# Pages spread over their ring slots by quarters, query products per column tile, scores and rope turned on VectorE, pair sums on column tiles

## What is computed

```python
def page_block(phys):
    kn, kr, v = mla_keys(cache_l[phys], w_uk, w_uv, k_norm_nope)
    return partial_softmax(mla_scores(qn, qr, kn, kr), v)
# kn = rms_norm(c @ w_uk) per head; scores = (qn . kn + qr . kr) * scale, over 8 heads
# partial_softmax: maximum over the tokens, exp, sum, and the sum weighted by v
```

## Time and profile before

| | |
|---|---|
| median of 3 runs | 1494.56 us |
| the profiled execution, its own time | 1494.17 us |
| its span, first to last instruction | 1492.4 us |
| PE busy | 1482.2 us, 99% |
| ACT busy | 880.6 us, 59% |
| DVE busy | 814.0 us, 55% |
| POOL busy | 216.6 us, 15% |
| share of PE in the chain that ended last | 96% |
| granted TensorE clock, mean | 0.999 |
| the page loop, first to last page's keys | 0.10 to 1.15 ms |

### The profile page before, as it was taken

One profiled execution on the slowest core, in us unless ns is written; L12 is line 12 of the kernel. 1 busy time (PEld: TensorE's weight loads), 2 busy tenths in 40 slices (PEclk: granted clock), 3 DMA queues, 4 the chain that ended last, 5 costly groups with the idle time before them and its releaser, 6 DMA issues.

```text
span 1492.4 us, 26962 instructions
## 1 busy us (share of the span) xinstructions
PE 1482.2 (99%) x9284; PEld 1221.2 (82%) x9284; DVE 814.0 (55%) x1596; ACT 880.6 (59%) x2836; POOL 216.6 (15%) x111
## 2 busy tenths in 40 slices
PE   9999999999999999999999999999999999999998
PEld 7877777867878778778777777778777999999998
DVE  5854444555455563555554555635433766787543
ACT  5545667686566675576855666755766454344332
POOL 3001111111131111111222111111312000000000
PEclk9999999999999999999999999999999999999999
DMA  9542315632245433255322463332644465555551
GB/s 284 169 116 36 77 44 125 157 82 61 63 99 135 114 81 73 60 127 135 83 61 61 101 151 80 63 68 61 162 106 121 149 211 206 168 171 176 185 183 58
DMA packets 263714, 173.92 MB, mean 117 GB/s; under 512 B 165464, under 2 KB 212088, under 8 KB 263448
## 3 DMA queue, kind: packets, MB, share of 16 engines
q1 hardware_dynamic: 263266, 171.94, 44.2%
q10 hardware_dynamic: 318, 0.33, 0.1%
HBM read 132.63 MB, written 6.74 MB: 93 GB/s over the span
## 4 chain that ended last, share of the span: by engine, by line
PE 96%; DVE 2%; ACT 1%; issue 0%; POOL 0%; DVEq 0%; ACTq 0%
PE ps L1991 17%; PE ps L1993 16%; PE ps L1992 16%; PE ps L2400 5%; PE ps L2401 5%; PE ps L2402 5%; PE ps L2031 2%; PE ps L2012 2%; PE ps L2084 2%; PE ps L2348 2%; PE ps L2349 2%; PE ps L2085 2%; PE ps L2086 2%; PE ps L2350 2%; PE ps L2150 2%; PE ps L2162 1%
## 5 line engine op out<-in xcount | busy, mean ns | idle before, releaser
L846 ACT ACTIVATE ksq<-ps 128x128 f32<-128x128 f32 x1024 | 268.9, 277 | 304.8 <-PE ps L1993 303.1
L1991 PE MATMUL ps<-ukh,cTh 128*128 128x512 f32 x1024 | 418.5, 409 | 0.3 <-DVE cTl L1233 0.3
L1993 PE MATMUL ps<-ukh,cTl 128*128 128x512 f32 x1024 | 401.3, 392 | 0.0
L1992 PE MATMUL ps<-ukl,cTh 128*128 128x512 f32 x1024 | 400.0, 391 | 0.0
L700 POOL TENSOR_TENSOR rk<-kss,mhalf 128x32 f32<-128x32 f32 x32 | 179.5, 5609 | 502.8 <-DVE kss L1659 502.8
L1991 PEld LDWEIGHTS ps<-ukh,cTh 128*128 128x128 f32 x1024 | 192.5, 188 | 55.4 <-issue 17.3
L1993 PEld LDWEIGHTS ps<-ukh,cTl 128*128 128x128 f32 x1024 | 192.2, 188 | 43.1
L1992 PEld LDWEIGHTS ps<-ukl,cTh 128*128 128x128 f32 x1024 | 192.9, 188 | 34.3
L846 ACT ACTIVATION_READ_ACCUMULATOR ksq<-ps 128x1 f32 x1024 | 211.6, 207 | 0.0
L834 ACT ACTIVATE cTr<-turned 128x1024 uint16<-128x1024 uint16 x126 | 173.6, 1378 | 9.6 <-PE ps L2015 6.9
L1035 ACT ACTIVATE wh<-wraw 128x2048 fp32r<-128x2048 f32 x44 | 84.3, 1916 | 131.7 <-PE ps L2402 127.2
(11 more groups left out here) (501 smaller groups left out, 2697.9 us busy)
## 6 DMA issues: line engine op xcount, KB each, us to landing
clat<-cache_mla SPq DMA_DIRECT2D x128, 256.0 KB, 2.6
wraw<-w_in SPq DMA_DIRECT2D x16, 1024.0 KB, 5.2
wraw<-w_up SPq DMA_DIRECT2D x16, 1024.0 KB, 5.4
wraw<-w_down SPq DMA_DIRECT2D x16, 1024.0 KB, 5.1
braw<-w_in SPq DMA_DIRECT2D x24, 512.0 KB, 4.0
crope<-cache_mla SPq DMA_DIRECT2D x128, 32.0 KB, 2.4
sst<-state_gdn SPq DMA_DIRECT2D x32, 128.0 KB, 3.2
gdn_sample<-sst SPq DMA_DIRECT2D x32, 128.0 KB, 2.1
```

The source lines that it names most:

```text
L846: i = nc.scalar.activation(ksq[:, P * h:P * h + P], ps[:, k % 3, P * h:P * h + P], ACT.Square, accum_out=kss[:, n // 4 % 2, n % 4, 4 * hal ...
L1991: mm(out, cTh[:, n % 2, c], ukh[:, c, cols], start=c == 0, stop=False)
L1992: mm(out, cTh[:, n % 2, c], ukl[:, c, cols], start=False, stop=False)
L1993: i = mm(out, cTl[:, n % 2, c], ukh[:, c, cols], start=False, stop=c == 3)
```

## The change

Five things are changed.

1. **Layout of the ring.** The four pages of a group are spread over the group's four slots: page `q` goes to partitions 32q to 32q+31 of all four, and slot `j` holds tokens 32j to 32j+31 of each page. Each load thus writes 32 partitions. One semaphore per group of slots counts all eight loads (`group_landed`).
2. **Scores.** `query_products` has for each latent chunk `c` four products, one per page `q` in column tile `q` (8 weight columns, 128 moving columns, 16 in all, the chunks summed in PSUM), and for the rope part eight with 32 rows each (`qro`). The result stands so that turning blocks of 32x32 gives a token to a partition: DVE does that in `score_parts` with one transpose straight from PSUM. `score_rows` (ACT) and `score_columns` (PE) are gone.
3. **Rope.** DVE `turned_rope` turns the rope part in blocks of 32x32 from `crope` to `rpT`; `rope_columns` (PE) and its copy (ACT) are gone. The queries' part `qro` is made once by 16 small products in `front_pe(2)`; two DMAs and a memset go.
4. **Places.** `split_planes` for page n+2 comes right behind `split_lo(n + 1)` in page n; it was at the end of page n-1. `turn` moves by one half page with it, the page loads from `i % 8 == 3` to 2, and `weigh` from the start of page t = 1 to the middle of page t = 0.
5. **Pair sums.** `l2r` and `osr` put each product's sum into a column tile of its own (32 weight columns), so the rows lie 32 apart, and `lb` is spread with 128 weight rows, `ob` with 64.

The diff, cut to its core:

```diff
-        qeff, e = place("qeff", [P, NS, 5, 16], F32, taken["rsq"][0])
+        qeff, e = place("qeff", [P, NS, 4, H], F32, taken["rsq"][0])
+        qro, e = place("qro", [P, NS, 2, H], F32, e)
         idr, e = place("idr", [P, P], F32R, e)
...
-        stp = ps[:, B_SCORE, :].rearrange("p (t n) -> p t n", t=4)
+        sparts = prows[:].rearrange("p (y x j r) -> p y x j r", y=2, x=2, j=4)
...
             def page(u, n):
                 pg = sp.value_load(ptab[0:1, bass.ds(n, 1)] if not isinstance(n, int) else ptab[0:1, n:n + 1], min_val=0, max_val=I["cache_mla"].shape[1] - 1)
                 rows_ = I["cache_mla"][0][bass.ds(pg, 1), :, :].rearrange("o p n -> p (o n)")
-                sp.dma_start(clat[:, u, :], rows_[:, 0:LAT]).then_inc(S(f"page_landed{u}"), 16)
-                sp.dma_start(crope[:, u, :], rows_[:, LAT:LW]).then_inc(S(f"page_landed{u}"), 16)
+                q, slots = u % 4, slice(u - u % 4, u - u % 4 + 4)
+                sp.dma_start(clat[32 * q:32 * q + 32, slots, :], rows_[:, 0:LAT].rearrange("(j a) n -> a j n", a=32)).then_inc(S(f"group_landed{u // 4}"), 16)
+                sp.dma_start(crope[32 * q:32 * q + 32, slots, :], rows_[:, LAT:LW].rearrange("(j a) n -> a j n", a=32)).then_inc(S(f"group_landed{u // 4}"), 16)
             def turn(n):
...
             sp.dma_start(O["conv_sample"][0, :, 0:CONVW - 2, :], I["state_conv"][0, :, 1:CONVW - 1, :]).then_inc(S("conv_shift"), 16)
             for i in range(2 * NT):
-                n = (i - 3) // 2 + RING - 8
-                if i % 8 == 3 and i >= 16 and n < NT:
+                n = (i - 2) // 2 + RING - 8
+                if i % 8 == 2 and i >= 16 and n < NT:
                     sp.wait_ge(S("pv_used"), i // 8 - 1)
                     for m in range(n, n + 4):
                         page(m % RING, m)
-                if i % 2 == 0 and i // 2 + 2 < NT:
+                if i % 2 == 1 and i // 2 + 2 < NT:
...
-            def turned_rope(gg):
-                act.wait_ge(S("rope_done"), gg + 1)
-                wait(act, "qk_done", gg)
-                nc.scalar.activation(rpT[:], ps[:, B_SCORE, 0:2 * P], ACT.Copy).then_inc(S("rope_ready"), 1)
-            def score_rows(gg):
-                act.wait_ge(S("qk_done"), gg + 1)
-                wait(act, "st_done", gg)
-                nc.scalar.activation(prows[:], ps[:, B_SCORE, :], ACT.Copy).then_inc(S("ssb_ready"), 1)
...
-                if t == 2:
-                    turned_rope(g)
-                if t == 3:
-                    score_rows(g)
                 beside(2 * n)
...
-            v.wait_ge(S("pool_clear"), 4)
+            v.wait_ge(S("pool_clear"), 3)
             def split_planes(n):
...
+            def turned_rope(gg):
+                wait(v, "qk_done", gg)
+                u = 4 * (gg % 3)
+                V.transpose(rpT[:], crope[:, u:u + 4, :].rearrange("p j n -> p (j n)")).then_inc(S("rope_ready"), 1)
             def score_parts(gg):
-                v.wait_ge(S("st_done"), gg + 1)
-                V.tensor_reduce(sparts[:, gg % 2].rearrange("p t a h -> p t (a h)"), stp.rearrange("p t (c n) -> p t n c", c=4)[:, :, 0:16, :], AX, ALU.add).then_inc(S("s_parts"), 1)
+                v.wait_ge(S("qk_done"), gg + 1)
+                V.transpose(sparts[:, gg % 2].rearrange("p x j r -> p (x j r)"), ps[:, B_SCORE, 0:256]).then_inc(S("s_parts"), 1)
...
+                V.tensor_tensor(ssc[:, y], sparts[:, y, 0, :, 0:H], rk[:, y], ALU.mult).then_inc(S("s_half"), 1)
...
-                V.tensor_tensor(ssc[:, y], sparts[:, y, :, 1, :], ssc[:, y], ALU.add).then_inc(S("s_ready"), 1)
+                V.tensor_tensor(ssc[:, y], sparts[:, y, 1, :, 0:H], ssc[:, y], ALU.add).then_inc(S("s_ready"), 1)
...
+                    V.tensor_scalar(lr[:, 0], bank("l2r")[:, 0:T], 1.0, EPS, ALU.mult, ALU.add).then_inc(S("a_read"), 1)
                 if k == 16:
...
                 if n + 1 < NT:
                     split_lo(n + 1)
+                if 1 <= n < NT - 2:
+                    split_planes(n + 2)
+                if t == 2:
+                    turned_rope(g)
                 if t == 0 and g >= 1:
                     score_parts(g - 1)
...
                 beside(2 * n + 1)
-                if n + 3 < NT:
-                    split_planes(n + 3)
                 if t == 2 and g >= 2 and g % 4 == 1:
...
             def transposes(n):
-                pe.wait_ge(S(f"page_landed{n}"), 32)
+                pe.wait_ge(S("group_landed0"), 128)
...
-                    pe.wait_ge(S(f"page_landed{u % RING}"), 32 * (u // RING) + 32)
-                wait(pe, "s_parts", gg)
-                for m in range(2):
-                    u = (4 * gg + 2 * m) % RING
-                    k = nc.tensor.transpose(ps[:, B_SCORE, P * m:P * m + P], crope[:, u:u + 2, :].rearrange("p u n -> p (u n)"), ident)
-                k.then_inc(S("rope_done"), 1)
             def query_products(gg):
...
                 s = gg // 4
                 pe.wait_ge(S("ct_raw"), 4 * gg + 4)
                 pe.wait_ge(S("rope_ready"), gg + 1)
-                pe.wait_ge(S("qeff_ready"), 1)
+                pe.wait_ge(S("a_read"), a_count("qcol1"))
                 wait(pe, "s_parts", gg)
                 for c in range(4):
-                    mm(ps[32 * c:32 * c + 16, B_SCORE, :], qeff[:, s, c, :], cTr[:, c, :], start=True, stop=False)
-                for t in range(4):
-                    r = slice(64 * (t % 2), 64 * (t % 2) + 64)
-                    k = mm(ps[32 * t:32 * t + 16, B_SCORE, P * t:P * t + P], qeff[r, s, 4, :], rpT[r, P * (t // 2):P * (t // 2) + P], start=False, stop=True)
+                    for q in range(4):
+                        mm(ps[32 * q:32 * q + H, B_SCORE, 0:P], qeff[:, s, c, :], cTr[:, c, :].rearrange("p (j q a) -> p q j a", q=4, a=32)[:, q], start=c == 0, stop=c == 3)
+                for x in range(2):
+                    for q in range(4):
+                        r = slice(32 * q, 32 * q + 32)
+                        k = mm(ps[32 * q:32 * q + H, B_SCORE, P:2 * P], qro[r, s, x, :], rpT[r].rearrange("p (j x a) -> p x j a", x=2, a=32)[:, x], start=x == 0, stop=x == 1)
                 k.then_inc(S("qk_done"), 1)
-            def score_columns(gg):
-                pe.wait_ge(S("ssb_ready"), gg + 1)
-                for t in range(4):
-                    k = nc.tensor.transpose(stp[:, t, :], prows[:, P * t:P * t + P], ident)
-                k.then_inc(S("st_done"), 1)
             def weigh(gg):
...
+                        i = mm(p_[32 * c:32 * c + 32, 0:T], window(0, 32), lsq[:, c, :], start=True, stop=True)
                     a_done(i)
                 if k in (15, 16):
...
+                        spread_row(f"lb{c}_{b}", P, 32 * c, lrh[:], lrl[:])
                 if k == 19:
...
                 if k == 46:
                     pe.wait_ge(S("row_rstd"), 2 * b + 2)
                     for hh in range(2):
...
             def front_pe(i):
                 def spread(out, x, n_, col):
...
+                    pe.wait_ge(S("qrs_ready"), 1)
+                    p_ = begin_a("qro")
+                    for x in range(4):
+                        for q in range(4):
+                            j = mm(p_[32 * q:32 * q + 32, 32 * x:32 * x + 32], consts[:, C_ID.start + 32 * x:C_ID.start + 32 * x + 32], qr[:, :, TP:T], start=True, stop=True)
+                    a_done(j)
                 if i in (3, 5):
...
                     transposes(1)
-                if t == 0 and g >= 1:
-                    score_columns(g - 1)
-                if t == 1 and g >= 2:
-                    weigh(g - 2)
-                if t == 2:
-                    rope_columns(g)
                 beside(2 * n)
                 keys(n, 0)
                 if t == 2 and g >= 2 and g % 4 == 1:
                     latent_columns(g // 4 - 1)
-                if n == NT - 1:
-                    score_columns(g)
+                if t == 0 and g >= 2:
+                    weigh(g - 2)
                 beside(2 * n + 1)
                 keys(n, 1)
```

More of the change, by code:

```diff
@@ L141 @@
 PAIR_B = ["cs", "rwA", "rwB", "vt", "kt", "ut1", "krow", "ut2", "urow", "ut3", "ut4", "ut5"]
-FRONT_A = ["ns", "rots", "qrow0", "qrow1", "rope0", "rope1", "qcol0", "qcol1", "rope2", "rope3", "rot0", "rot1", "rot2", "rot3", "snew"]
+FRONT_A = ["ns", "rots", "qrow0", "qrow1", "qro", "rope0", "rope1", "qcol0", "qcol1", "rope2", "rope3", "rot0", "rot1", "rot2", "rot3", "snew"]
 FRONT_A += [f"nope{h % 2 * H + h // 2}" for h in range(2 * H)]
@@ L271, in build @@
         qk, o = place("qk", [P, 2, H, NS], F32, o)
-        qr64, o = place("qr64", [P, 4, NS], F32, o)
         assert o <= 212800, o
@@ L303, in build @@
         assert e <= C_NEG.stop * 4
-        lrl, e = place("lrl", [8, T], F32R, taken["krT"][0] + 4 * T)
-        lr, e = place("lr", [8, 2, T], F32, taken["krT"][0])
+        lrl, e = place("lrl", [P, T], F32R, taken["krT"][0] + 4 * T)
+        lr, e = place("lr", [P, 2, T], F32, taken["krT"][0])
         assert e <= taken["decay_raw"][1]
```

(4 more changed lines are left out.)

47 lines of the change are left out of this document (15 added, 32 removed).

## The result

| | before | changed |
|---|---|---|
| median of the runs | 1494.43 (1494.01 to 1494.81, 4 runs) | 1512.6 (1511.28 to 1517.82, 4 runs) |
| ratio, with 95% interval | | 1.0128 (1.011 to 1.0147) |
| profiled run: time, span | 1494.17, 1492.4 | 1513.33, 1511.5 |
| TensorE without a matmul in the span | 10.2 | 39.3 |
| mean granted clock | 0.999 | 0.992 |

The forecast was 1475.6, with 1487 as the upper end. It is wrong by 37 us, and in sign.

The account below looks back on a forecast made before the run. The prediction took TensorE's own stream to bound the kernel, busy 1482.2 of 1492.4 us. Terms of -22.0 us on TensorE and +3.0 at the loop's end gave -19.0: 1475.6 us for the median, range 1469 to 1487.

Parts of the forecast that it names:

- The price list of TensorE: TensorE's own steps, priced from the timeline: work added and removed comes to -22.0 us without the other engines.
- l2r, osr and lb together: Pair sums on TensorE: l2r -5.3 us, osr -1.8 us, lb -3.0 us.
- The query products: TensorE, once per group: latent part costs nothing more, rope part about +0.21 us a group, +6.7 us in all.
- Rival C: TensorE's products of 32 rows and 8 columns do not run side by side: +42 us, 1518; chance 0.07.
- The other engines: ACT, DVE, SP and loads: the page loop has slack on average; only its end costs, +3.0 us (0 to 8).
- Rival B: Page preparation binds in the whole loop as the transposing DMA takes a microsecond more: 1488 us; chance 0.10.
- its two signs: In the profile: keys waiting for `cTl` all along the loop, and `cTr` waiting over a few microseconds for the transposing DMA.
- The loop of 6.6 us: `cTl`, `planes`, transposing DMA, `cTr`, `cTh`: some 6.6 us per page against 8.2 on average, without slack from page 116 on.
- the lead of `cTl`: In the last pages `cTl` is ready 3.0 us ahead of its keys, to be used up before TensorE waits.
- SP adds perhaps 0.5: SP issues eight page loads between two turns: perhaps 0.5 us in each of three groups at the end.
- They stand behind `cTl` and `planes`, so no page waits for them: DVE's two new transposes of 128x256, at most 1.4 us per group, are covered and cost nothing.
- No cost: Page loads writing 32 partitions: even at twice 2.6 us they land over 6 us ahead of their group's first `planes` copy.

Follow-up runs that it names:

- e12: The changed kernel with planes late only for page 4g+4, the other three pages at their old places, and page loads on SP behind the transposition: 1479.42 us.
- e9: e8 with planes and transposition of three pages in four back at their old places, only page 4g+4 half a page later: 1478.1 us.
- e4: The kernel before with only the pair sums changed (l2r, osr, lb, ob in their new form): 1484.49 us.
- e5: The kernel before with only planes and the transposition at their late places, page loads ahead of the transposition of page 4g+3: 1520.75 us.
- e3: The changed kernel with query_products(g) moved on TensorE behind the first half of the keys of page 4g+3: 1573.29 us.
- e8: e6 with the page loads of SP's loop issued from GpSimd's queue: 1497.38 us.
- e11: e5 with the page loads on SP behind the transposition of page 4g+3 instead of ahead of it: 1513.54 us.
- e6: The changed kernel with the rope's turn (turned_rope) moved on VectorE ahead of split_lo and split_planes: 1503.76 us.
- e10: e6 with planes late only for page 4g+4, and page loads on SP behind the transposition: 1479.11 us.
- e1: The changed kernel with planes and the transposition at their old places for all pages, page loads behind the transposition: 1508.46 us.
- e14: The kernel before with TensorE held at the start of page 4g+3 in eight groups until GpSimd wrote 22 scratch columns: 1563.11 us.
- e15: The kernel before with TensorE held at the start of page 4g+3 in 24 groups until GpSimd wrote 7 scratch columns: 1637.16 us.

## Why the prediction was wrong

**The price list of TensorE was right.** The terms gave -22.0 us of work. e12 has 24.0 us less busy time and e9 23.3, of which the mean clock of e12, 1.000 for 0.999, may be 1.5. Of its parts, l2r, osr and lb together were -10.1 and measured -9.7 (e4). The query products were to be 1.51 + 0.21 = 1.72 us per group; an undisturbed group of the changed kernel has 707.44 - 705.25 = 2.19, less 0.46, 1.73:

```profile
705.25 0.39 PE L1977 MATMUL ps<-ukh,cTl 128*128 128x512 f32 x1
705.57 1.06 PE L1989 MATMUL ps<-cTr,qeff 128*8 128x128 f32 x32
706.56 0.62 PE L1993 MATMUL ps<-rpT,qro 32*8 32x128 f32 x16
707.11 0.50 PE L1975 MATMUL ps<-ukh,cTh 128*128 128x512 f32 x1
707.44 0.39 PE L1976 MATMUL ps<-ukl,cTh 128*128 128x512 f32 x1
```

Rival C, products of 32 rows one after the other, is out: 16 passes in 0.55 us from start to start. The 48 passes take 1.54 us, 32 ns each with all their changes of shape. The Trainium skill's rule (page "TensorEngine Tiling (Array Packing)", section "Instruction Overhead") of some 60 cycles for each matmul would, as an estimate from that page, make the 32 passes more dearer by 0.8 us a group (25 ns each). The trace does not agree: the new form is 0.22 us dearer than the old one (1.73 against 1.51).

**The step that failed is "The other engines".** It said of the late copy to `planes`: "The page loop lasts 1.05 ms for 128 pages, 8.2 us each, and on average the loop has slack", and priced the end of the loop at +3.0 us, between 0 and 8. Alone it costs +26.6 (e5). Rival B named this mechanism, with a chance of 0.10 and a price of 12 us. One of its two signs came: ACT's `cTr` waits 78.2 us for the transposing DMA. The other, PE's keys waiting for `cTl` all along the loop, did not: that is 1.3 us in 2 waits, and PE waits at the query products. Four mistakes stand in the section:

1. The loop of 6.6 us was right and its slack was not. In the last groups `planes` follows `planes` in 6.87 and 6.67 us, then 9.15, 6.79 and 8.08:

```profile
1110.75 0.69 DVE L1209 COPY planes<-clat 128x1024 uint16<-128x1024 uint16 x1
...
1117.62 0.69 DVE L1209 COPY planes<-clat 128x1024 uint16<-128x1024 uint16 x1
...
1124.29 0.69 DVE L1209 COPY planes<-clat 128x1024 uint16<-128x1024 uint16 x1
...
1133.44 0.69 DVE L1209 COPY planes<-clat 128x1024 uint16<-128x1024 uint16 x1
...
1140.23 0.69 DVE L1209 COPY planes<-clat 128x1024 uint16<-128x1024 uint16 x1
...
1148.31 0.68 DVE L1209 COPY planes<-clat 128x1024 uint16<-128x1024 uint16 x1
```

The 9.15 is the page whose transposition stands behind the loads: 2.3 to 2.5 us more than the two ahead of it, where I gave 0.5. It was issued 1.6 us later than it could be and took 4.2 us to land instead of 3.1. The 8.08 is another thing: there the transposition landed in 3.1 us, and `cTr` started 1.6 us behind the landing. From 1117.62 to 1148.31, four pages, it is 30.7 us, where the pages of before last 25.3.

2. One deadline was overlooked. I took the lead of `cTl` over the keys of its page, 3.0 us. But `query_products(g)` needs `cTr` of page 4g+3 and stands ahead of the keys of that page; and ACT may write `cTr` of page 4g+4 only behind these products. A late page 4g+3 is handed on to the next one through the products. e3 shows this edge at its strongest, 126.6 us. It isn't the only one: in e8, where PE hardly waits at the products, the late chain still costs 19.3 us, and in e11 8.3 us are at the score columns.

3. The other work of SP and VectorE was averaged. SP is behind not by its share of time but by what stands ahead of one transposition: at 652 eight page loads and a load of the pair, 7.1 us. The wait of 3.94 us is this, and "SP adds perhaps 0.5" was meant for the end of the loop alone.

4. "They stand behind `cTl` and `planes`, so no page waits for them" leaves out the query products, which wait for `rpT`: 8.8 us (e6) with the chain late, 0.3 with the chain in time (e12 against e10).

**"No cost" for the load's new layout was right as placed and hid the reason for the placing.** Loads landed in 3.0 us instead of 2.6:

```profile
clat<-cache_mla SPq DMA_DIRECT2D x128, 256.0 KB, 3.0
```

The Trainium skill ("SBUF — State Buffer", section "Door 1: The DMA port swizzle") has 32 partitions reach half of the ports; here this was 0.4 us a load and nothing like twice the time. What the layout costs is that a group is usable only when all of it has landed. With `planes` at its old place VectorE stands 88.2 us (e1, +29.3 over e10, of which the rope's place is 2.7 at most); half a page later for one page in four, 9.4 us (e10) or less. The change paid for this with a late place for all four pages, and three of them didn't need it.

**And a long wait costs more than itself.** No term allowed for the clock. The four long waits brought 20.4 us (2 x 3.4 + 2 x 6.8) at the 1.2 GHz level, 18.4 of them busy, and half of that is 9.2 us, a third of what the waits themselves cost. Of the 13.3 us of added busy time (1472.2 against 1458.9 in e9) some 4 stay unexplained. The Trainium skill says the same of another kernel ("TensorE: Matmul & The Clock Gate", section "HAM oscillation — how this bites in real kernels"): waits for DMA send TensorE to its lower clock, and the price is half the time spent there. The traces of e14 and e15 agree, with 18.1 and 47.3 us of added busy time for 38.5 and 100.5 us of busy time at that level.

The end on the slower side thus came from B, and not from C, where I had put it. B's price was 12 us because it let longer pages give back half; the nested runs show 19.3 + 6.4 = 25.7 us for it, and the 8.8 of the rope's place, which no rival had, on top: 34.5, the whole distance from e9.

## What to carry to other kernels

When a copy is moved later in a software pipeline, don't ask whether the mean loop has slack: follow the one item with the earliest consumer (here page 4g+3, wanted by the query products ahead of its own keys), and add up what stands ahead of it in each in-order queue, DMA issues included, and see what stands behind it. If a new data layout makes one item in four wait for more, delay that item and leave the others where they are: here this is the difference between 1512.6 and 1479.4 us. And price a wait of TensorE of 3 us and more at its length and about 2 us more, on average.

## What the runs showed of the hardware

- A wait of TensorE costs more than its length. The 32 waits of 1.7 to 9.1 us in e14 and e15 brought 2.0 to 2.3 us of added busy time each, on average, and 29 of them a stretch of 3.4, 6.8 or 10.2 us with the granted clock at 0.50. One of these in e14, with PEclk 1.00, 0.50, 1.00:

```profile
625.00:632.00 7.00, 2.49 (x11) 1.70 (x10) 1.08 (x2) 1.18 (x9) 3.38 (x1) 1.00 0.20 37
632.70:635.90 3.20, 3.20 (x20) 1.10 (x16) 0.00 (x0) 0.74 (x1) 0.00 (x0) 0.50 0.00 0
636.00:643.00 7.00, 7.00 (x40) 6.05 (x40) 3.73 (x9) 3.47 (x14) 0.00 (x0) 1.00 0.00 0
```

- A turn of 128x256 elements on VectorE takes 0.44 us, from SBUF (`rpT`) as from PSUM (`prows`), less than the copy of 128x1024 halves at 0.69; two are 0.88 us a group, where my bound was 1.4.
- GpSimd issued a page load in some 1.2 us for its two DMAs (614 and 572 ns in e8), and in e9 these landed in 4.4 us instead of 3.0. e9 is no slower than e10 for it: with the chain in time neither the longer landing nor SP's queue counts for more than 1.0 us.

```profile
clat<-cache_mla POOLq DMA_DIRECT2D x112, 256.0 KB, 4.4
```
